# A two-layer hybrid backbone on one core: early conditioning weights in 2 KB rows, and the retention keys and queries as a 512-column pair

## What is computed

```python
shift, scale, gate = split(silu(cond) @ w_ada[l] + b_ada[l], 3)    # cond: c_ctx for context, c for latent
h = rms_norm(x, norm_gain[l]) * (1 + scale) + shift
z = h @ w_in[l]                       # 1024 x 4096; 16 parts of 256 columns: A conv, B attention, C retention, D attention
y_a, y_b, y_c, y_d = conv(z), gqa(z), retention(r_q, r_k, r_v), diff_attention(z)
merged = sum(sigmoid(h @ w_mgate[l])[:, i] * ((y_i * silu(gate_i)) @ w_branch[l][i]))
x = x + gate * (merged @ w_out[l])
```

## Time and profile before

| | |
|---|---|
| median of 3 runs | 1365.81 us (1364.88 to 1368.04) |
| profiled execution | 1364.36 us, of which its span is 1362.4 us |
| PE busy | 1330.2 us, 98% of the span |
| DVE, ACT, POOL busy | 883.9, 567.1, 78.2 us |
| DMA | 127.62 MB, mean 94 GB/s |

### The profile page before, as it was taken

The page is one execution under the profiler, slowest core; times in us unless marked ns, Lnnn a source line. Parts: engine busy times, 40 slices in busy tenths (PEclk is TensorE's granted clock), DMA queues, the critical chain, the costliest instruction groups (busy, mean ns, idle before and its releaser), DMA issues.

```text
span 1362.4 us, 25807 instructions
## 1 busy us (share of the span) xinstructions
PE 1330.2 (98%) x9623; PEld 1265.8 (93%) x9623; DVE 883.9 (65%) x1801; ACT 567.1 (42%) x1252; POOL 78.2 (6%) x99
## 2 busy tenths in 40 slices
PE   5999999999999999999999999999999999999997
PEld 2899999989999999999889999999999999999986
DVE  2587786457665588867875777655766557654455
ACT  2676665234553222223354666532445423222241
POOL 1000000010000000100010000001100000001000
PEclk9999999999999999999999999999999999999999
DMA  9522212223103433365442212112221143214322
GB/s 319 176 63 67 78 40 71 63 64 100 32 32 98 136 109 101 109 168 181 137 158 67 67 40 78 40 63 78 78 71 32 46 155 112 78 40 125 124 78 78
DMA packets 106352, 127.62 MB, mean 94 GB/s; under 512 B 4125, under 2 KB 92793, under 8 KB 106233
## 3 DMA queue, kind: packets, MB, share of 16 engines
q1 hardware_dynamic: 102040, 112.33, 25.8%
q0 software_dynamic: 4192, 13.65, 3.3%
HBM read 119.66 MB, written 6.31 MB: 92 GB/s over the span
## 4 chain that ended last, share of the span: by engine, by line
PE 92%; DVE 4%; ACT 1%; issue 1%; DMA 1%; SPq 0%; POOL 0%; DVEq 0%; ACTq 0%; POOLq 0%
PE G L1576 45%; PE G L1574 13%; PE G L1572 11%; PE BK L1591 8%; PE TO L1691 3%; PE TP L1677 3%; PE S L1668 2%; PE TP L1648 1%; PE BK L1606 1%; PE TP L1718 1%; PE TP L1636 1%; PE S L1670 1%; PE TO L1710 1%; PE S L1671 1%; PE S L1624 1%
## 5 line engine op out<-in xcount | busy, mean ns | idle before, releaser
L1576 PE MATMUL G<-h_hi,w_hi 128*128 128x320 f32 x1472 | 249.8, 312 | 0.0
L1576 PE MATMUL G<-h_hi,w_lo 128*128 128x320 f32 x1472 | 248.7, 311 | 0.0
L1576 PE MATMUL G<-h_lo,w_hi 128*128 128x320 f32 x1472 | 246.7, 310 | 0.0
L1199 DVE TENSOR_TENSOR w_lo<-w_raw,w_hi 128x512 fp32r<-128x512 f32 x312 | 205.8, 685 | 52.3 <-ACT w_hi L968 52.1
L1576 PEld LDWEIGHTS G<-h_lo,w_hi 128*128 128x128 f32 x1472 | 222.9, 188 | 0.0
L1576 PEld LDWEIGHTS G<-h_hi,w_hi 128*128 128x128 f32 x1472 | 221.3, 188 | 1.2 <-issue 0.7
L1576 PEld LDWEIGHTS G<-h_hi,w_lo 128*128 128x128 f32 x1472 | 222.0, 188 | 0.0
L968 ACT ACTIVATE w_hi<-w_raw 128x512 fp32r<-128x512 f32 x312 | 182.5, 623 | 54.9 <-DMA w_raw<-in_w_branch 32.6
L1063 ACT ACTIVATE tg<-G 128x320 f32<-128x320 f32 x128 | 55.6, 435 | 210.2 <-PE G L1576 204.4
L1108 ACT ACTIVATE work<-S,neg_max 128x640 f32<-128x640 f32 (+1 forms) x120 | 85.1, 710 | 124.1 <-DVE neg_max L1388 108.4
L1306 DVE SCALAR_TENSOR_TENSOR tg<-tg,BK 128x320 f32<-128x320 f32 x96 | 46.7, 487 | 116.7 <-PE BK L1591 98.6
(11 more groups left out here) (251 smaller groups left out, 1848.2 us busy)
## 6 DMA issues: line engine op xcount, KB each, us to landing
w_raw<-in_w_mgate SPq DMA_DIRECT2D x32, 1024.0 KB, 5.4
w_raw<-in_w_in SPq DMA_DIRECT2D x29, 1024.0 KB, 5.4
w_raw<-in_w_ada SPq DMA_DIRECT2D x17, 1024.0 KB, 5.2
w_raw<-in_w_branch SPq DMA_DIRECT2D x32, 256.0 KB, 5.7
w_raw<-in_w_out SPq DMA_DIRECT2D x8, 1024.0 KB, 5.2
early_raw<-in_w_ada SPq DMA_DIRECT2D x6, 1024.0 KB, 12.1
work<-gate_rows POOLq DMA_DIRECT2D x4, 512.0 KB, 5.1
za<-in_x_prompt POOLq DMA_DIRECT2D x2, 512.0 KB, 8.7
```

The lines of the kernel that those rows point to most:

```text
L1199: V.tensor_tensor(w_lo[:, s.n % 2, a:b, :], raw_rows(s), w_hi[:, s.n % 2, a:b, :].bitcast(F32), ALU.subtract).then_inc(lo_done, 1)
L1576: ins = mm(g[:, 0:HALF], a[:, w, kt, c], b[:, kt, half], start=first, stop=last)
```

## The change

The eight early loads become row blocks: 512 columns of one half of the rows (4 x 128 rows), so 1 MB as before, with 2 KB in a row instead of 1 KB. The order is column blocks 0, 2, 1, 3 (256-column chunks 0-1, 4-5, 2-3, 6-7), for each the upper and then the lower half of the rows. `ada` makes 4 matmuls of 512 columns; only after the second half is the bank copied, by two copies, to `ada_rows`, which now lies in `tg`, and turned by two `adat` steps. The quarters of `h` are made in two pairs, the first pair after the second column block and the second pair after the last.

The retention's keys and queries are made by `wide`, keys first. The chunks that host a `later` part change: the queries' chunk no longer does, the last gate chunk of mixer D (`branch == 3`) does.

```diff
-    order = [0, 4, 1, 5, 2, 6, 3, 7]
-    early = [Step("asplit", l=0, c=c, q=1) for c in order]
+    early = [Step("asplit", l=0, c=a, half=kh, q=1) for a in (0, 2, 1, 3) for kh in range(2)]
...
-        p6 = [tok("w_in", C_K, "ck"), tok("w_in", C_Q, "cq"), tok("w_in", C_V, "cv"), feat(C_GATE, "gate")]
+        p6 = wide("w_in", (C_K, "ck"), (C_Q, "cq"), 0)
+        p6b = [tok("w_in", C_V, "cv"), feat(C_GATE, "gate")]
...
-                return [Step("adat", l=0, c=order[2 * j + 1]), *[Step("warm", part=WARM_TURN - (j < 3))] * (j > 1), Step("scales", l=0, part=j), Step("hquarter", l=0, part=j)]
+                return [Step("adat", l=0, c=4 + j, part=j % 2), *[Step("warm", part=WARM_TURN)] * (j == 2), Step("scales", l=0, part=j), Step("hquarter", l=0, part=j)]
...
-                if i % 2:
-                    body += [Step("adat", l=0, c=order[i - 1])]
-                elif i:
-                    body += quarter(i // 2 - 1)
-                body += [Step("hearly", l=0, t=1)] * (i == 4)
-                body += [Step("ada", l=0, c=c, of=early[i])] + [Step("warm", part=WARM_ADA)] * (i in (5, 6))
+                if i in (2, 6):
+                    body += [Step("adat", l=0, c=i // 2 - 1 + p, part=p) for p in range(2)]
+                elif i == 4:
+                    body += quarter(0) + quarter(1)
+                body += [Step("hearly", l=0, t=1)] * (i == 5)
+                body += [Step("ada", l=0, half=i % 2, of=early[i])] + [Step("warm", part=WARM_ADA)] * (i in (5, 6))
...
-            body += [p1[0][0]] + [Step("xfirst", l=0, t=2)] + first[:2] + quarter(3) + first[2:]
+            body += [p1[0][0]] + [Step("xfirst", l=0, t=2)] + quarter(2) + first[:2] + quarter(3) + first[2:]
...
-        u = units(p6)
+        u = p6 + units(p6b)
         u[0] = u[0] + ysplits("B")
-        body += flat(u[:45])
-        body += spread(u[45:] + units(p7), retention_groups(l))
+        body += flat(u[:33])
+        body += spread(u[33:] + units(p7), retention_groups(l))
...
-            host = (c.src == "w_in" and C_Q <= c.col < D_Q) or c.branch == 1 or (c.branch == 2 and c.col % DM) or \
+            host = (c.src == "w_in" and c.col in (C_K, C_V, C_GATE)) or c.branch == 1 or \
+                (c.branch == 2 and c.col % DM) or (c.branch == 3 and c.col % DM == 3 * CW) or \
                 (c.src == "w_out" and c.col == CW)
...
-        ada_rows = sb("ada_rows", [P, CW])
+        ada_rows = tg[:, :, :].rearrange("p a b -> p (a b)")[:, 0:512]
...
                 if k == "ada":
+                    if s.half == 0:
+                        continue
                     dve.wait_ge(ada_used, s.a + 1)
                     dve.wait_ge(to_done, s.before["to"])
-                    V.tensor_copy(ada_rows[:, :], BK[:, 0:CW]).then_inc(bk_evac, 1)
+                    for part in range(2):
+                        V.tensor_copy(ada_rows[:, part * CW:(part + 1) * CW], BK[:, part * CW:(part + 1) * CW]).then_inc(bk_evac, 1)
...
-                    for kt in range(KT):
-                        r = 32 * (kt % 4)
-                        ins = mm(BK[r:r + 32, 0:CW], cond_w[:, 2 * kt:2 * kt + 32], raw[:, kt, :], start=kt < 4, stop=kt >= 4, tile_position=(0, r))
+                    raw = ada_half(s.of)
+                    for i in range(4):
+                        kt, r = 4 * s.half + i, 32 * i
+                        ins = mm(BK[r:r + 32, :], cond_w[:, 2 * kt:2 * kt + 32], raw[:, i, :], start=s.half == 0, stop=s.half == 1, tile_position=(0, r))
```

More of the change, by code:

```diff
@@ L242, in quarter @@
             def quarter(j):
-                return [Step("adat", l=0, c=order[2 * j + 1]), *[Step("warm", part=WARM_TURN - (j < 3))] * (j > 1), Step("scales", l=0, part=j), Step("hquarter", l=0, part=j)]
-            for i, c in enumerate(order):
+                return [Step("adat", l=0, c=4 + j, part=j % 2), *[Step("warm", part=WARM_TURN)] * (j == 2), Step("scales", l=0, part=j), Step("hquarter", l=0, part=j)]
+            for i in range(len(early)):
                 body += [early[i]]
@@ L460, in number @@
                 n["mod"] = n["tg"]
-            else:
+            elif k == "branch":
                 n["bkd"] += 1
+            elif s.half:
+                n["bkd"] += 2
         if k == "gate" or (k == "zfeat" and s.dest in ("gate", "agate")):
@@ L547, in number @@
                 n[k] += 1
+        if k == "adat":
+            s.rows_need = n["bkd"] - 1 + s.part
         if k in ("ysplit", "adat"):
@@ L740, in raw_chunk @@
         def raw_chunk(s):
-            w = t_in["w_ada" if s.kind == "asplit" else s.src][s.l]
-            col = s.c * CW if s.kind == "asplit" else s.col
-            return w[:, col:col + CW].rearrange("(k p) c -> p k c", p=P)
+            return t_in[s.src][s.l][:, s.col:s.col + CW].rearrange("(k p) c -> p k c", p=P)
         block = ctx.enter_context(nc.Block())
@@ L766, in _ @@
                         sp.wait_ge(ada_added, s.last.last_use)
-                    if s.kind == "asplit" and s.q == 0:
+                    if s.kind == "asplit":
                         sp.dma_start(ada_half(s), t_in["w_ada"][s.l][4 * P * s.half:4 * P * (s.half + 1), 512 * s.c:512 * s.c + 512]
@@ L1602, in _ @@
                     pe.wait_ge(raw_in[s.of.slot], s.of.raw_target)
-                    raw = raw_slot(s.of.slot)
-                    for kt in range(KT):
-                        r = 32 * (kt % 4)
-                        ins = mm(BK[r:r + 32, 0:CW], cond_w[:, 2 * kt:2 * kt + 32], raw[:, kt, :], start=kt < 4, stop=kt >= 4, tile_position=(0, r))
+                    raw = ada_half(s.of)
+                    for i in range(4):
+                        kt, r = 4 * s.half + i, 32 * i
+                        ins = mm(BK[r:r + 32, :], cond_w[:, 2 * kt:2 * kt + 32], raw[:, i, :], start=s.half == 0, stop=s.half == 1, tile_position=(0, r))
                     ins.then_inc(ada_used, 1)
@@ L1610, in _ @@
                         pe.wait_ge(to_evac, s.to)
-                    pe.wait_ge(bk_evac, s.before["bkd"])
+                    pe.wait_ge(bk_evac, s.rows_need)
                     for b in range(2):
-                        ins = nc.tensor.transpose(TO[:, b * P:(b + 1) * P], ada_rows[:, b * P:(b + 1) * P], ident)
+                        at = s.part * CW + b * P
+                        ins = nc.tensor.transpose(TO[:, b * P:(b + 1) * P], ada_rows[:, at:at + P], ident)
                     ins.then_inc(to_done, 1)
```

## The result

| | before | after |
|---|---|---|
| median | 1365.32 us of 6 (1363.94 to 1368.04) | 1360.66 us of 6 (1359.41 to 1361.90) |
| ratio after/before | | 0.9963, 95% interval 0.9953 to 0.9973 |
| profiled execution, its span | 1364.36, 1362.4 us | 1361.90, 1360.1 us |

The change is worth 5.0 us by the ratio (4.7 by the two medians), where the forecast was 2.5. The time of 1360.66 lies just under the range of 1361.0 to 1365.6. It is odd at first sight that the two profiled executions differ by 2.46 us, just what the sum says. The profiled execution of after is the slowest of its six, and that of before is one of its quickest.

The account below looks back on a forecast made before the run. PE was taken to bound the kernel, with copies, turns and quarters of h carrying the early stage. The pair's 2.5 us and an even early stage gave 1365.81 - 2.5 = 1363.3 us, range 1361.0 to 1365.6.

Parts of the forecast that it names:

- the sum: Whole kernel: profiled execution 1364.36 - 2.5 for the pair + 0.0 for the early stage = 1361.9 us.
- The pair: Retention's keys and queries, both layers: each 512-column matmul saves 13 ns over two narrow ones, 2.5 us in all.
- (c): Retention: the hosted part makes DVE late for the pair, or its handover waits; + 0.5 us a layer, 1364.3; chance 0.07.
- (d): Retention pair: the fixed time of a matmul is not saved; gain only 0.5 us, 1365.3; chance 0.04.
- The chain to the last weight product: Early stage: second load lands at 13.1, then products, turns and two quarters; last weight product at 31.8, 2.1 us gained.
- The early stage comes out even: Up to the first product with w_in: the tail gives back the chain's gain, 37.7 against 37.66; bounds 36.7 and 38.6.
- So DMA sets only the start of the chain: Early stage before: the eighth load lands 1.6 us ahead of its product; copies, turns and quarters of h carry it.
- The tail: Last weight product to first product with w_in: two quarters in a row make it 5.9 us instead of 3.78.
- (a): Early stage also faster: DMA over 372, clock up before the turn of x, first product at 36.7; 1362.1 us; chance 0.22.
- (b): First tiles: PE's clock falls after the idle tail; + 1.2 us, 1364.5; chance 0.13.
- (e): Early stage: clock stays at 1.2 GHz from 18 to 42 us; + 7.5 us, 1370.8, slower; chance 0.06.
- before 36.5: Sign in the early stage: the forecast is wrong if the first product with w_in starts before 36.5 or after 39.

Follow-up runs that it names:

- eight profiled executions, 5 to 8: The last four of eight profiled executions of the unchanged kernel before: 1366.51, 1367.81, 1365.76 and 1366.05 us, first products at 39.82, 41.18, 39.10 and 39.44.
- the 59 executions above: Executions of the unchanged kernel before in two comparisons and its run against itself: mean clock 0.997 in 24 (1363.8 to 1365.2 us), 0.995 in 11, 0.998 or 0.999 in 24.
- the repeat: The changed kernel, after, unaltered and run once more beside the others, with a second profile: 1360.21 us, ratio 0.9957 to before.
- the tail experiment: After with ACT rounding two pieces of w_in's first chunk ahead of the last two quarters of h, DVE's low parts of both last: 1359.68 us, ratio 0.9954 to before.
- execution 6: Sixth profiled execution of the unchanged kernel before: 1367.81 us, first product with w_in at 41.18, mean clock 0.999.
- execution 5: Fifth profiled execution of the unchanged kernel before: 1366.51 us, first product with w_in at 39.82, mean clock 0.995.
- executions 7 and 8: Seventh and eighth profiled executions of the unchanged kernel before: 1365.76 and 1366.05 us, first products with w_in at 39.10 and 39.44, mean clock 0.999.

## Why the prediction was wrong

**The pair: right.** 21.79 us for 96 matmuls as in the rows of mixer B, no wait of PE, DVE in time, and alone it brings 2.8 us (1.5 to 3.8) against 2.5. Rivals (c) and (d) fall. Behind the first product the profiles say 2.7 (once 2.3). The rule of the Trainium skill that the prediction weighed ("TensorE: Matmul & The Clock Gate", Back-to-back issue gap) would have given 0.5 us, which is outside that interval; but the skill gives it for an isolated matmul and says that a stream has another spacing, so I had set it against rows for which it is not meant.

**The step that failed: from the profiled execution to the median.** The sum ended in "the median of the runs lies 1.45 above the profiled one, so the forecast is 1365.81 - 2.5". I carried those 1.45 us over to after as if they were spread that any kernel has. They are PE's clock in the early stage of before: four of its eight profiled executions, 5 to 8, have PE at its lower level for longer than in the profile I read, up to 34 us. 35 of the 59 executions above are in the same two groups by time and mean clock; only those four were profiled, so for the 35 it is inferred. The usual first product of before is at 1365.9 - 1326.7 = 39.2, not 37.66. The earlier trace rows had shown one lucky case of this mechanism, and I priced the clock as a cost of the change only, never as something that the change could give back. The times given (1364.88 to 1368.04, against 1364.36 profiled) were a hint: three executions all slower than the profiled one.

**The chain to the last weight product: right in form, three terms too long.** In the first profile of after it ended at 31.76, forecast 31.8, but that is its slowest execution, and the fit is partly luck: the first two turns took 0.25 us less than I added (the second follows the first within 0.64 us in both profiles of after, so DVE's scaling of x was not in its way), and the turn of x 0.3 more than the 1.64 I had. In the repeat: the second load's product starts at 12.59, not 13.1 (it stands 2.62 us behind the first load's product in both profiles, at 387 GB/s and not 372, but that one started at 9.97 instead of 10.62); the product behind the turn of x takes 1.27, not 1.94, since PE is up to speed in it; the tail is 5.71, not 5.9. That is 0.5 + 0.65 + 0.2 = 1.35 us, and 37.7 - 1.35 = 36.35 against 36.25 measured. Together with the 1.5 us of before this is the miss: 1363.3 - 1.5 - 1.35 = 1360.5. The 1.35 are those of the quicker of two executions. By its median the usual first product of after is at about 1360.66 - 1323.96 = 36.7, 1.0 ahead of the forecast (an estimate).

**"The early stage comes out even": wrong**, by these two. Alone it brings 3.1 us (2.0 to 4.4). How much of it is the clock and how much the 2 KB rows has no single answer in the runs. Counted with the clock first: constants take 2.0 us off the span of the old stage (1363.75 to 1361.8), and the new stage alone is another 0.9 under that (1360.9). By device time the two steps are 1.2 and 1.7, but the first has 0.7 us outside its span against it. Counted with the order first: the new order with 1 KB rows brings 0.7 us (1363.11 to 1362.43, both with the pair), the rows 1.9 more. The steps depend on each other: with 1 KB rows a fast PE waits for its last load, 0.86 us in the old order and 1.32 in the new, so each of the two changes is worth more when the other is there. That denser work of PE in the new order is what brings the clock up sooner fits its profiles, but was not tested by itself. "So DMA sets only the start of the chain" held for the profiled execution alone.

The Trainium skill ("DMA: Bandwidth & Descriptors", Where 436 GB/s comes from) says that for HBM to SBUF "the HBM side (~358) binds". By it the 348 GB/s of before left next to nothing to gain; the trace disagrees, at 387 GB/s over 10 us. The same page's table of measured rates (Measured) has 425 GB/s for 16 MB by a single core and about 358 for each of two cores that stream at once; with one core at work, the trace fits that better.

**The tail: right**, 5.71 us in both profiles against 5.9, and the tail experiment moved it by 0.86 us, where its chain says 1.0.

**Rivals.** (a), 1362.1, is what happened in the main: DMA above 372 and the clock up earlier, though not before the turn of x as it asked (1.97 us in both profiles of after) but in the product behind it. Its size was too small because it too was counted from the profiled execution. (b) did not show in the two profiles of after (clock 1.00 from 22 to 40 us), but it did in after with two constants, at about 1.2 us inside the span, as priced. (e) fell: in both profiles of after products take 1.06 or 1.07 us from the one at 23.95 or 25.17 on. Of the signs to look for, the first product "before 36.5" was named as what would prove the forecast wrong, and the repeat's 36.25 is that; the first profile, at 37.47, shows none of these signs.

## What to carry to other kernels

Before you add a median's distance from the profiled execution to a forecast, ask which stage makes it: here time less the start of the first steady product was the same to 0.1 us in eight executions, so all of the spread was in the first 40 us, and the change was about to remove most of it. A stage in which PE is slow at first and then waits in lumps landed here on either clock level from one execution to the next; price the clock on both sides of the change, as a gain too. And a load that has landed in good time while PE is slow may be the bound once PE is fast: add the chain up at both levels before you call it hidden. Last, compare spans beside device times: here one kernel lost 0.7 us outside its span, which hid a third of what its constants gained inside.

## What the runs showed that I had not expected

- The recorded clock does not show the slow start. In execution 6 the record is 1.00 from the start on while products take 1.94 us, as they do at the lower level in execution 5 (recorded 0.50 in 26 to 30 us), until 34 us; executions 7 and 8 are the same until 28 us. Where the record falls below 1.00 in these traces, PE has been fast once before (execution 5). So two groups with a mean of 0.999 and 0.995 are both slow in the early stage, and the one with 0.997 is the quick one. The Trainium skill ("TensorE: Matmul & The Clock Gate", Seeing it yourself) warns that the clock's trace events can be unreliable; the durations of equal rows decide.
- Queued loads from 10 to 20 us run at 348 and 349 GB/s with 1 KB rows, in either order, and at 387 with 2 KB rows: 11% more, where single loads had let me guess 7%.
- Four matmuls on constants (2.15 us of PE in its idle stretch ahead of 22.3 us) narrowed the spread of before from 4.2 to 1.4 us (the spans from 4.2 to 1.1).
